# Neighbourhood attention by pairs of heads in row tiles, with a moved first pair and a moved group of channel sums

## The chip, the cores and the metric

The kernel runs on one core of one Trainium2 chip, as a hand-written program for its engines: TensorE (PE, whose weight loads are listed as PEld), VectorE (DVE), ScalarE (ACT), GpSimd (POOL) and SyncE (SP). The metric is the device time of one execution in microseconds; the value shown is the median of several runs.

## The reference, cut to what matters

The whole computation is a hybrid layer (a state-space part and a forgetting attention) on 272 tokens, and then, on 256 tokens, two layers that each hold a convolution module, a neighbourhood attention, a feed-forward part (dense in layer 0, a mixture of eight experts in layer 1) and norms. All is float32. The change touches the two neighbourhood attentions and the channel norm of the convolution that runs between them.

```python
def neighbourhood_attention(q, k, v, rpb):       # 8 heads of 64, a grid of 4 rows of 64 columns
    scale = Dh ** -0.5
    ...
    s = jnp.einsum("bjqhd,bijkhd->bhjqik", q_row, k_band).astype(jnp.float32) * scale
    s = jnp.where(col_mask[:, :, None, :], s + bias.astype(jnp.float32), -jnp.inf)
    w = jax.nn.softmax(s.reshape(B, H, N_CB, Q_CB, kr * BAND_C), axis=-1)
    return jnp.einsum("bhjqik,bijkhd->bjqhd", w, v_band)

def conformer_conv(a, g, w, b, ln_g, ln_b):
    u = a * jax.nn.sigmoid(g)
    y = lax.conv_general_dilated(u, w[:, None, :], ...)   # 31 taps, 512 channels
    y = layer_norm(y + b, ln_g, ln_b)                     # over the 512 channels
    return jax.nn.silu(y)

def hybrid_stack(h):
    for i in range(2):
        proj = h @ w_in[i] + b_in[i]          # a, g, q, k, v of 512 columns each
        conv_out, attn_out = conformer_conv(...), neighbourhood_attention(...)
        mix = jnp.concatenate([conv_out, attn_out], axis=-1) @ w_out[i] + b_out[i]
        h = layer_norm(ALPHA * h + mix, ...)
        ...
```

With 256 tokens in four grid rows every query sees all four rows, so a head's scores for 128 queries are a 128 x 256 tile, to which a table of biases (`tb`, with -1e30 where a column is outside the window) is added.

## The kernel before

Every engine runs its own instruction list in the order in which it is written, and waits on semaphores, which the helper `wait(engine, name, value)` names. `S["x"].on(instruction)` makes an instruction count up semaphore x. There is no scheduler: what stands behind a waiting instruction on an engine waits too. TensorE alone may load weights ahead.

Weights come in chunks of 1 MB through a ring of six places by DMAs that SP issues when TensorE has released a place (`give`, `chunks_used`). Each large product is made of three passes: ACT rounds a chunk to a high part (L1516 and others), DVE makes the rest (L2040), and TensorE multiplies high x high, high x rest, rest x high (`split_product`, listed at L642).

In each of the two layers (`layer(i)` of the three engines) `features` computes the projections of gate, values of the convolution, keys and queries in blocks f of 128 columns: f = 8 to 11 are keys, 12 to 15 queries. ACT's `keys(f)` (L1823, L1827) moves a block out of its bank with its bias. Keys lie in `k2` with two heads per tile of 128 partitions; queries lie in `q2` with one tile per head, of which DVE's `zero_halves` has set the other head's half to zero, so that a score matmul over 128 partitions takes one head. Between blocks 14 and 15 `conv_mean` (L1205) sums the convolution's output over channels; DVE subtracts the mean (L2516) and ACT squares it (L1858).

Then comes the attention, as u = 0 to 15: u // 8 is the half of the queries (128 each), u % 8 the head. For each u:
- TensorE `scores2(u)` (L1217): 128 x 256 scores into one of three banks;
- DVE: scale and add of the bias (L2523), then the negated row maximum (L2527), into one of three places of `sc2`;
- ACT: exponential with the sum over the row (L1863);
- TensorE `turn2(u)` (L1224): two 128 x 128 transposes;
- ACT `copy_t` (L1915): the transposed weights into `p2T`;
- TensorE `weigh2(u)` (listed at L642 with 128x64 outputs): two products with the values.

TensorE's order is a software pipeline: at step u it runs scores2(u), turn2(u - 2), weigh2(u - 3). Into it are put `conv_spread` (L1242, sums of squares over channels, at u = 2), `conv_scale` (L1249, at u = 9), and `turn_a(0)` (L1256, transposes of the first half's output, at u = 15). On DVE the steps that belong to them are an ask for an inverse root to POOL (u == 4), the diagonal tiles (L2535, u == 6), the scaling of the convolution (L2540, u == 10) and `attended(0)`, the division by the row sums (L2509, L2511, u == 11). After the 16 steps come the products with w_out, "the mix", whose first matmul reads the transposed and split first half (`copy_a`, L1870, and `rest_a`, L2547).

The attention of the hybrid layer, earlier in the same kernel, is written in another form, which the diff takes over: `scores(p)` (L940 adds a decay row, L945 the scores) runs two heads as two matmuls over 64 partitions each, on the upper and lower half of the array's rows; DVE does addition, negation and minimum in one `tensor_tensor_reduce` (L2284); `turn_p` (L955) does the transposes of both heads, DVE copies them together (L2294), and `weigh` (L975) follows.

## Time and profile before

| | us |
|---|---|
| median of 3 runs | 2062.36 (2062.07 to 2062.44) |
| the profiled execution | 2061.95 |
| its span | 2060.3 |

| engine | busy us | share of span | instructions |
|---|---|---|---|
| PE | 2035.3 | 99% | 10989 |
| PEld | 1699.0 | 82% | 10989 |
| DVE | 1579.0 | 77% | 1430 |
| ACT | 1269.3 | 62% | 1272 |
| POOL | 163.2 | 8% | 134 |

The granted clock of TensorE is at its full level in all 40 slices of the span. A busy TensorE is not one at its peak, since matmuls overlap and their ends are modelled; what counts is the distance from one start to the next. The chain of waits goes back from the last instruction, at each step to what released it or to the instruction before it on its engine. In a timeline consecutive instructions of a kind are one line with their count.

### The profile page before, as it was taken

The page shows a single profiled execution, that of the slowest core. Times are in us where ns is not written, and L with a number is a line of the kernel's source. Part 1 is how long each engine was busy: PE and PEld are TensorE (multiplying, and loading weights), DVE is VectorE, ACT ScalarE, POOL GpSimd, SP SyncE. Part 2 cuts the span into 40 slices and gives each one's busy share as a digit, 9 for nine tenths or more (in the row PEclk, how much of TensorE's full clock was granted, in tenths as well). Part 3 has the DMA queues.
Part 4 walks back from the last instruction along what each step waited for, and adds up shares of the span by engine and source line. Part 5 has one row for each costly group of instructions (what it writes and reads, how often), then busy time and mean ns, then how long its engine had stood idle before and what let it go on. Part 6 is the DMA issues. An engine that isn't in the chain of part 4 may idle for free.

```text
span 2060.3 us, 29349 instructions
## 1 busy us (share of the span) xinstructions
PE 2035.3 (99%) x10989; PEld 1699.0 (82%) x10989; DVE 1579.0 (77%) x1430; ACT 1269.3 (62%) x1272; POOL 163.2 (8%) x134
## 2 busy tenths in 40 slices
PE   9999999999999999999999999999999999999998
PEld 8977897778889998987778888888888888888876
DVE  7767544687666557679988888888888888888897
ACT  7666433453644334466677777777777777777674
POOL 0031010000214000021400000000000000000100
PEclk9999999999999999999999999999999999999999
DMA  6533594237555555726999999999999999999995
GB/s 254 186 103 105 196 358 169 83 131 261 159 185 202 189 185 187 255 90 228 358 412 383 367 384 370 371 380 368 382 370 381 368 371 380 368 382 370 383 381 211
DMA packets 88065, 580.41 MB, mean 282 GB/s; under 512 B 10144, under 2 KB 13472, under 8 KB 22064
## 3 DMA queue, kind: packets, MB, share of 16 engines
q1 hardware_dynamic: 79472, 548.26, 70.7%
q0 software_dynamic: 7904, 29.95, 4.0%
q8 instruction: 57, 0.93, 0.2%
q10 hardware_dynamic: 608, 1.07, 0.2%
q14 instruction: 24, 0.20, 0.0%
HBM read 559.96 MB, written 15.73 MB: 279 GB/s over the span
## 4 chain that ended last, share of the span: by engine, by line
PE 91%; DVE 4%; DMA 1%; issue 1%; ACT 1%; POOL 0%; DVEq 0%; ACTq 0%; SPq 0%
PE bank L642 84%; PE bank L1414 1%; DMA ring<-in_w_moe 1%; DVE wrest L2634 1%; PE bank L857 1%; PE bank L1217 1%; DVE wrest L2040 0%; DMA cst<-in_consts 0%; PE bank L860 0%; PE bank L1385 0%; PE bank L1031 0%; PE bank L945 0%; PE bank L975 0%; PE bank L1224 0%; ACT ohi L1737 0%
## 5 line engine op out<-in xcount | busy, mean ns | idle before, releaser
L2634 DVE TENSOR_TENSOR wrest<-ring,whi 128x2048 fp32r<-128x2048 f32 x378 | 853.7, 2304 | 77.7 <-ACT whi L1939 77.3
L1939 ACT ACTIVATE whi<-ring 128x2048 fp32r<-128x2048 f32 x374 | 699.2, 1918 | 84.1 <-DMA ring<-in_w_moe 82.0
L642 PE MATMUL bank<-whi,xgT 128*128 128x512 f32 x1008 | 404.7, 402 | 3.0 <-DVE wrest L2634 3.0
L642 PE MATMUL bank<-wrest,xgT 128*128 128x512 f32 x1008 | 396.3, 393 | 0.0
L642 PE MATMUL bank<-whi,xgR 128*128 128x512 f32 x1008 | 393.5, 390 | 0.0
L642 PEld LDWEIGHTS bank<-whi,xgT 128*128 128x128 f32 x1008 | 189.5, 188 | 47.3 <-DVE wrest L2634 7.1
L642 PEld LDWEIGHTS bank<-whi,xgR 128*128 128x128 f32 x1008 | 189.5, 188 | 46.6
L642 PEld LDWEIGHTS bank<-wrest,xgT 128*128 128x128 f32 x1008 | 188.9, 187 | 38.7
L642 PE MATMUL bank<-whi,hidE 128*128 128x512 f32 x504 | 201.8, 400 | 0.8 <-DVE wrest L2634 0.8
L642 PE MATMUL bank<-wrest,hidE 128*128 128x512 f32 x504 | 197.8, 392 | 0.0
L642 PE MATMUL bank<-whi,hidR 128*128 128x512 f32 x504 | 196.8, 390 | 0.0
L642 PE MATMUL bank<-hTh,wrest 128*128 128x256 f32 x608 | 171.4, 282 | 0.0
L1954 ACT ACTIVATE arena<-bank 128x512 f32<-128x512 f32 x63 | 37.6, 597 | 179.1 <-PE bank L642 179.1
L2040 DVE TENSOR_TENSOR wrest<-ring,fhi 128x2048 fp32r<-128x2048 f32 x33 | 76.5, 2317 | 81.8 <-ACT fhi L1516 81.8
L642 PEld LDWEIGHTS bank<-hTh,wrest 128*128 128x128 f32 x608 | 114.6, 188 | 0.0
L642 PEld LDWEIGHTS bank<-whi,hidR 128*128 128x128 f32 x504 | 94.7, 188 | 23.6
L642 PEld LDWEIGHTS bank<-whi,hidE 128*128 128x128 f32 x504 | 94.6, 188 | 22.6 <-DVE wrest L2634 2.3
L1516 ACT ACTIVATE fhi<-ring 128x2048 fp32r<-128x2048 f32 x33 | 63.0, 1913 | 78.0 <-PE bank L642 78.0
L642 PEld LDWEIGHTS bank<-wrest,hidE 128*128 128x128 f32 x504 | 94.4, 187 | 20.1
L2040 DVE TENSOR_TENSOR wrest<-ring,lhi 128x2048 fp32r<-128x2048 f32 x20 | 45.9, 2293 | 71.4 <-ACT lhi L1524 71.4
L642 PE MATMUL bank<-hTh,fhi 128*128 128x256 f32 x352 | 99.4, 282 | 0.0
L642 PE MATMUL bank<-hTr,fhi 128*128 128x256 f32 x352 | 99.0, 281 | 0.0
(483 smaller groups left out, 3688.5 us busy)
## 6 DMA issues: line engine op xcount, KB each, us to landing
ring<-in_w_moe SPq DMA_DIRECT2D x378, 1024.0 KB, 4.9
ring<-in_w_dense SPq DMA_DIRECT2D x135, 1024.0 KB, 4.8
row<-in_rows POOLq DMA_DIRECT2D x17, 512.0 KB, 5.2
xg_rows<-ncR POOLq DMA_DIRECT2D x12, 512.0 KB, 25.2
y_rows<-arena POOLq DMA_DIRECT2D x9, 512.0 KB, 6.2
arena<-xg_rows SPq DMA_DIRECT2D x9, 512.0 KB, 5.4
arena<-arena SPq DMA_DIRECT2D x32, 106.5 KB, 3.8
arena<-in_tbias POOLq DMA_DIRECT2D x2, 1536.0 KB, 8.8
```

Of the source, the lines that this page charges most:

```text
L642: ins = pe.matmul(out_, lhsT, rhs, start=start, stop=stop, **more)
L857: ins = pe.matmul(ps[5][:, r * HD:(r + 1) * HD], dec[:, j, r * P:(r + 1) * P], xdt[:, j, r * HD:(r + 1) * HD], start=True, stop=True, skip ...
L1217: S["s_ps"].on(pe.matmul(score_bank(u), q2[:, hh, j * P:(j + 1) * P], k2[:, hh // 2, :], start=True, stop=True))
L1414: ins = pe.transpose(ps[4][:, b * P:(b + 1) * P], hid[:, b * P:(b + 1) * P], ident)
L1516: S["w_hi"].on(a.activation(hi, ring[:, c % RING, :], ACT.Copy))
L1939: S["w_hi"].on(a.activation(whi[:, n % HI_SLOTS, :], ring[:, c % RING, :], ACT.Copy))
L1954: S["m_sl"].on(a.activation(sle, ps[0][:, :], ACT.Silu))
L2040: S["w_lo"].on(v.tensor_tensor(wrest[:, s, :], ring[:, s, :], hi.bitcast(F32), ALU.subtract))
L2634: S["w_lo"].on(v.tensor_tensor(wrest[:, s, :], ring[:, s, :], whi[:, n % HI_SLOTS, :].bitcast(F32), ALU.subtract))
```

## The change

Four things are changed in both layers. (1) Queries are kept as keys are, two heads per tile, scaled by 1/8 when they are moved out; `zero_halves` is gone, and DVE scales the query bias once. Scores, transposes and weighings go by pairs p = 0 to 7: two score matmuls over 64 partitions in row tiles, four transposes into one bank, one copy of 128 x 512, four products. (2) On DVE one `tensor_tensor_reduce` takes the place of two operations, into four places; the copies of pairs 0, 1, 3, 6, 7 are DVE's, those of 2, 4, 5 ACT's. (3) The scores of pair 0 stand between the query blocks 14 and 15, behind `conv_mean`; on ACT `keys(15)` is moved behind the first two exponentials. (4) `conv_spread` is moved from before the first transposes to behind the weighing of pair 0; the steps of the norm on DVE move to u = 6, 8, 11 and `attended(0)` to u = 13.

```diff
@@ -59,6 +59,7 @@
 START_FILL = 12
+DVE_COPIES, ACT_COPIES = (0, 1, 3, 6, 7), (2, 4, 5)
 AHEAD = 4
@@ -245,8 +246,8 @@
         cc, rdiag = at(9792, 4, SEQ), at(24064, 2, P)
-        k2, q2, v2 = at(10816, 4, SEQ), at(11840, N_HEADS, SEQ), at(26624, 2, 512)
-        sc2, p2T, o2 = at(13888, 3, SEQ), at(14656, 2, SEQ), at(15168, 2, 512)
+        k2, q2, v2 = at(10816, 4, SEQ), at(11840, 4, SEQ), at(26624, 2, 512)
+        sc2, p2T, o2 = at(12864, 4, SEQ), at(13888, 2, 512), at(15168, 2, 512)
         tb = at(16384, N_HEADS, 6 * GRID_W)
@@ -394,6 +395,12 @@
             return 5 * (q + 1)
+
+        def copied(i, p):
+
+            for name, copies, first in (("pt_done", DVE_COPIES, meta_count(3)), ("t_done", ACT_COPIES, 0)):
+                if p in copies:
+                    return name, first + len(copies) * i + copies.index(p) + 1
@@ -1205,33 +1212,44 @@
-                features(14, 16, conv_mean)
-                wait(pe, "p_act", 12 * i + 11)
-
-
-                def scores2(u):
-                    j, hh = divmod(u, N_HEADS)
-                    if u == 2:
+                def scores2(p):
+                    if p == 1:
                         wait(pe, "cn_done", 3 * i + 1)
-                    wait(pe, "s_in", 16 * i + max(u - 2, 0))
-                    S["s_ps"].on(pe.matmul(score_bank(u), q2[:, hh, j * P:(j + 1) * P], k2[:, hh // 2, :],
-                                           start=True, stop=True))
-
-                def turn2(u):
-                    wait(pe, "s_exp", 16 * i + u + 1)
-                    wait(pe, "t_done", 16 * i + max(u - 1, 0))
-                    for b in range(2):
-                        ins = pe.transpose(ps[2 + u % 2][:, b * P:(b + 1) * P], sc2[:, u % 3, b * P:(b + 1) * P],
-                                           ident)
+                    wait(pe, "s_in", 16 * i + max(2 * p - 1, 0))
+                    for u in (2 * p, 2 * p + 1):
+                        j, hh = divmod(u, N_HEADS)
+                        r = slice(HD * (u % 2), HD * (u % 2) + HD)
+                        S["s_ps"].on(pe.matmul(score_bank(u), q2[r, hh // 2, j * P:(j + 1) * P], k2[r, hh // 2, :],
+                                               start=True, stop=True))
+
+                def conv_mean_and_scores():
+                    conv_mean()
+                    wait(pe, "p_act", 12 * i + 10)
+                    scores2(0)
+
+                features(14, 16, conv_mean_and_scores)
+
+
+                def turn2(p):
+                    wait(pe, "s_exp", 16 * i + 2 * p + 2)
+                    if p >= 2:
+                        wait(pe, *copied(i, p - 2))
+                    for u in (2 * p, 2 * p + 1):
+                        for b in range(2):
+                            x = 2 * (u % 2) + b
+                            ins = pe.transpose(ps[2 + p % 2][:, x * P:(x + 1) * P], sc2[:, u % 4, b * P:(b + 1) * P],
+                                               ident)
                     S["t_ps"].on(ins)
...
-                def weigh2(u):
-                    j, hh = divmod(u, N_HEADS)
-                    c = slice(hh * HD, (hh + 1) * HD)
-                    wait(pe, "t_done", 16 * i + u + 1)
-                    for b in range(2):
-                        ins = mm(ps[4 + j][:, c], p2T[:, u % 2, b * P:(b + 1) * P], v2[:, b, c],
-                                 start=b == 0, stop=b == 1, skip_group_check=True)
+                def weigh2(p):
+                    wait(pe, *copied(i, p))
+                    for u in (2 * p, 2 * p + 1):
+                        j, hh = divmod(u, N_HEADS)
+                        c = slice(hh * HD, (hh + 1) * HD)
+                        for b in range(2):
+                            x = 2 * (u % 2) + b
+                            ins = mm(ps[4 + j][:, c], p2T[:, p % 2, x * P:(x + 1) * P], v2[:, b, c],
+                                     start=b == 0, stop=b == 1, skip_group_check=True)
                     S["a_ps"].on(ins)
@@ -1256,23 +1274,24 @@
-                for u in range(19):
-                    if u == 3:
-                        wait(pe, "p_act", 12 * (i + 1))
-                    if u < 16:
-                        scores2(u)
-                    if u == 2:
-                        conv_spread()
-                    if u == 9:
+                for p in range(1, 10):
+                    if p in (2, 3):
+                        wait(pe, "p_act", 12 * i + 9 + p)
+                    if p < 8:
+                        scores2(p)
+                    if p == 5:
                         conv_scale()
-                    if u == 15:
+                    if p == 8:
                         wait(pe, "cn_done", 3 * (i + 1))
                         turn_a(0, 7)
-                    if 2 <= u <= 17:
-                        turn2(u - 2)
-                    if u >= 3:
-                        weigh2(u - 3)
-                wait(pe, "t_done", 16 * (i + 1))
+                    if p <= 8:
+                        turn2(p - 1)
+                    if p >= 2:
+                        weigh2(p - 2)
+                    if p == 2:
+                        conv_spread()
+                wait(pe, *copied(i, 6))
+                wait(pe, *copied(i, 7))
                 wait(pe, "s_in", 16 * (i + 1))
@@ -1822,10 +1841,8 @@
                     else:
-                        for e in range(2):
-                            r = slice(e * HD, (e + 1) * HD)
-                            ins = a.activation(q2[r, 2 * (f - 12) + e, :], ps[f % 4][r, 0:SEQ], ACT.Identity,
-                                               bias=bias[r])
+                        ins = a.activation(q2[:, f - 12, :], ps[f % 4][:, 0:SEQ], ACT.Identity, bias=bias,
+                                           scale=HD ** -0.5)
                     S["p_act"].on(ins)
@@ -1856,14 +1873,15 @@
                 S["cq_done"].on(a.activation(csq[:, :, :], cc[:, :, :], ACT.Square))
-                keys(15)
                 for u in range(16):
+                    if u == 2:
+                        keys(15)
                     j, hh = divmod(u, N_HEADS)
                     wait(a, "s_in", 16 * i + u + 1)
-                    S["s_exp"].on(a.activation(sc2[:, u % 3, :], sc2[:, u % 3, :], ACT.Exp,
+                    S["s_exp"].on(a.activation(sc2[:, u % 4, :], sc2[:, u % 4, :], ACT.Exp, scale=-1.0,
                                                bias=nmax[:, u % 4:u % 4 + 1], accum_out=rsum[:, j, hh:hh + 1]))
-                    if u:
-                        copy_t(i, u - 1)
+                    if u % 2 == 0 and u // 2 - 1 in ACT_COPIES:
+                        copy_t(i, u // 2 - 1)
@@ -1879,7 +1897,6 @@
                 copy_a(0, 7)
-                copy_t(i, 15)
                 wait(a, "cn_done", 3 * (i + 1))
@@ -1909,10 +1926,10 @@
-            def copy_t(i, u):
-                wait(a, "t_ps", 16 * i + u + 1)
-                wait(a, "a_ps", 16 * i + max(u - 1, 0))
-                S["t_done"].on(a.activation(p2T[:, u % 2, :], ps[2 + u % 2][:, 0:SEQ], ACT.Copy))
+            def copy_t(i, p):
+                wait(a, "t_ps", 8 * i + p + 1)
+                wait(a, "a_ps", 8 * i + max(p - 1, 0))
+                S["t_done"].on(a.activation(p2T[:, p % 2, :], ps[2 + p % 2][:, :], ACT.Copy))
@@ -2204,12 +2221,6 @@
                 S["t_lo"].on(v.tensor_tensor(yTr[:, t, :], yT[:, t, :], yTh[:, t, :].bitcast(F32), ALU.subtract))
-
-            def zero_halves(q):
-
-                pairs = q[:, :, :].rearrange("p (f e) n -> p f e n", e=2)
-                v.memset(pairs[HD:P, :, 0, :], 0.0)
-                fin(v.memset(pairs[0:HD, :, 1, :], 0.0))
@@ -2476,7 +2487,8 @@
                 rest_proj(i, 4)
-                zero_halves(q2)
+                q_bias = vec[:, v0 + VL_BK + 4:v0 + VL_BK + 8]
+                v.tensor_scalar(q_bias, q_bias, HD ** -0.5, None, ALU.mult)
                 rest_proj(i, 5)
@@ -2507,7 +2519,7 @@
                     fin(v.reciprocal(rinv[:, j, 0:8], rsum[:, j, 0:8]))
-                    wait(v, "a_ps", 16 * i + 8 * (j + 1))
+                    wait(v, "a_ps", 8 * i + 4 * (j + 1))
                     S["a_ready"].on(v.tensor_tensor(o2[:, j, :].rearrange(c3, r=8), ps[4 + j][:, :].rearrange(c3, r=8),
@@ -2516,31 +2528,37 @@
                 v.wait_ge(tb_in, 16 * (i + 1))
+                def copy_t(p):
+                    wait(v, "t_ps", 8 * i + p + 1)
+                    wait(v, "a_ps", 8 * i + max(p - 1, 0))
+                    S["pt_done"].on(v.tensor_copy(p2T[:, p % 2, :], ps[2 + p % 2][:, :]))
+
                 for u in range(16):
...
                     wait(v, "s_ps", 16 * i + u + 1)
-                    wait(v, "t_ps", 16 * i + max(u - 2, 0))
-                    fin(v.scalar_tensor_tensor(sc2[:, u % 3, :], score_bank(u), HD ** -0.5,
-                                               tb[:, hh, (2 - 2 * j) * GRID_W:(6 - 2 * j) * GRID_W],
-                                               ALU.mult, ALU.add))
+                    wait(v, "t_ps", 8 * i + max(u // 2 - 1, 0))
                     wait(v, "s_exp", 16 * i + max(u - 3, 0))
-                    S["s_in"].on(v.tensor_reduce(nmax[:, u % 4:u % 4 + 1], sc2[:, u % 3, :], AX.X, ALU.max,
-                                                 negate=True))
-                    if u == 4:
+                    S["s_in"].on(v.tensor_tensor_reduce(sc2[:, u % 4, :], score_bank(u),
+                                                        tb[:, hh, (2 - 2 * j) * GRID_W:(6 - 2 * j) * GRID_W], -1.0, 3e38,
+                                                        ALU.add, ALU.min, nmax[:, u % 4:u % 4 + 1]))
+                    if u % 2 and u // 2 - 1 in DVE_COPIES:
+                        copy_t(u // 2 - 1)
+                    if u == 6:
                         wait(v, "cv_ps", 3 * i + 2)
                         asked = ask_inv_sqrt(rs[:, 6:8], ps[7][:, 0:2], 1.0 / CONV_CH, LN_EPS)
-                    if u == 6:
+                    if u == 8:
                         wait(v, "pow_done", asked)
...
                         S["cn_done"].on(ins)
-                    if u == 10:
+                    if u == 11:
                         wait(v, "cv_ps", 3 * i + 3)
...
                                                          ALU.mult))
-                    if u == 11:
+                    if u == 13:
                         attended(0)
+                copy_t(7)
                 def rest_a(j, bank):
```

## Rows read from the trace of the kernel before

**Rows 1.** The page, part 4: the chain that ended last, by engine.
```profile
PE 91%; DVE 4%; DMA 1%; issue 1%; ACT 1%; POOL 0%; DVEq 0%; ACTq 0%; SPq 0%
```

**Rows 2.** Chain of waits about layer 0's attention: start us, length us, what.
```profile
482.16 59.35 PE bank L642 x576
...
543.24 2.85 PE bank L642 x24
...
547.39 1.68 PE bank L1242 x16
...
554.62 0.39 PE bank L642 x4
555.02 0.49 PE bank L1217 x2
555.50 0.22 PE bank L1224 x2
...
556.60 0.43 PE bank L1249 x2
...
571.34 16.65 PE bank L642 x72
```

**Rows 3.** The same chain in layer 1.
```profile
877.41 2.85 PE bank L642 x24
...
905.50 16.65 PE bank L642 x72
```

**Rows 4.** Timeline, layer 0: start us, length, engine, line, operation [idle before <-releaser].
```profile
544.67 1.06 ACT L1858 ACTIVATE arena<-arena 128x1024 f32<-128x1024 f32 x1 [2.17 <-DVE arena L2516]
...
547.10 1.28 ACT L1863 ACT_TABLE_LOAD   x1
...
562.62 0.51 ACT L1863 ACTIVATE arena<-arena,nmax 128x256 f32<-128x256 f32 x1 [0.75 <-DVE nmax L2527]
...
563.27 0.44 PE L1224 MATMUL bank<-cst,arena 128*128 128x128 f32 x2 [0.21 <-ACT arena L1863]
...
567.88 0.47 PE L642 MATMUL bank<-aside,catH 128*128 128x512 f32 x1
```

**Rows 5.** Groups by form, 538 to 572 us: busy us, mean ns | idle before, releaser.
```profile
L2523 DVE SCALAR_TENSOR_TENSOR arena<-bank,arena 128x256 f32<-128x256 f32 x16 | 6.7, 421 | 5.1 <-PE bank L1217 5.0
...
L2527 DVE TENSOR_REDUCE nmax<-arena 128x1 f32<-128x256 f32 x16 | 6.7, 420 | 0.6
...
L1827 ACT ACTIVATE arena<-bank,vec 64x256 f32<-64x256 f32 x4 | 1.9, 470 | 0.8 <-PE bank L642 0.8
```

**Rows 6.** Timeline of the first block's attention, which is by pairs in row tiles.
```profile
399.26 0.73 PE L945 MATMUL bank<-arena 64*128 64x272 f32 x4
399.93 0.66 PE L955 MATMUL bank<-cst,arena 128*128 128x128 f32 x4
400.02 0.44 DVE L2284 CUSTOM_DVE_ANT_0 arena<-bank,causal 128x272 f32<-128x272 f32 x1 [0.70 <-PE bank L945]
...
400.42 1.00 PE L975 MATMUL bank<-arena 128*128 128x64 f32 x8
400.51 0.52 ACT L1720 ACTIVATE arena<-arena,nmax 128x272 f32<-128x272 f32 x1 [1.68 <-DVE nmax L2284]
...
400.75 0.69 DVE L2294 COPY arena<-bank 128x512 f32<-128x512 f32 x1
...
401.03 0.51 ACT L1720 ACTIVATE arena<-arena,nmax 128x272 f32<-128x272 f32 x1
...
401.23 0.50 PE L940 MATMUL bank<-ncR,picked 128*128 128x272 f32 x2
```

**Rows 7.** By line: its durations, min/median/max ns.
```profile
L945 PE MATMUL bank<-arena x64: 282/388/493, 373.6 to 413.2; 64*128 64x144 f32 x32, 64*128 64x272 f32 x32
...
L1710 ACT ACTIVATE yaTh<-bank x4: 576/577/582, 396.2 to 426.5; 128x512 fp32r<-128x512 f32 x4
...
L2569 DVE TENSOR_TENSOR arena<-arena,bank x8: 686/688/690, 579.8 to 926.6; 128x512 f32<-128x512 f32 x8
```

## Prediction

> **What bounds the kernel now.** I read the page's chain first: 91% of it is TensorE [rows 1], so an edit counts only as far as it shortens TensorE's own sequence or a gap in it. Next the chain of waits around the place that changes. Before it, TensorE runs one unbroken stretch of 59.35 us [rows 2], so ACT or DVE work that is saved there (the two memsets of zero_halves, the halved `keys` activations of queries) buys nothing: it lies beside that stretch. From 543.24 the last query block takes 2.85 us, and from 546.09 to 567.88, when the first matmul of the mix starts [rows 2, 4], comes the neighbourhood attention: 21.79 us. In layer 1 the distance from the last query block (877.41) to the long mix stretch (905.50) is 28.09 us; in layer 0 it is 571.34 - 543.24 = 28.10 [rows 2, 3]. So one calculation does for both layers.
>
> Inside, a head costs TensorE 0.49 (score) + 0.22 (two transposes) + 0.39 (weighing) = 1.10 us [rows 2]. Sixteen heads are 17.60; the sums of squares take 1.68, conv_scale 0.43 [rows 2] and turn_a four transposes, 0.44: together 20.15. The remaining 1.64 us are gaps, late in the stage, where DVE's two operations per head and its conv work make it late: 5.0 us of DVE's idle time wait for scores [rows 5], and an exponential starts after 0.75 us of ACT idling, with the transposes behind it 0.65 later [rows 4].
>
> **The change, part by part.** The best witness for the new form is the first block's attention, which already runs by pairs in row tiles, with the same one-pass DVE operation.
>
> Scores. Two K=64 matmuls of four instructions at 272 columns take 399.93 - 399.26 = 0.67 from first start to the transposes [rows 6]; with 256 columns an estimate of 0.64. That is more than half of two full-array scores (0.98, [rows 2]), so the tiles overlap only in part. Bounds: 0.49 (full overlap) and 0.98 (none).
> Transposes. Four take 400.42 - 399.93 = 0.49, weighing a pair 401.23 - 400.42 = 0.81 [rows 6], against 0.44 and 0.78 for two heads now: grouping is slightly dearer here. A pair costs 0.64 + 0.49 + 0.81 = 1.94 against 2.20; eight pairs 15.52 against 17.60, so 2.08 us of TensorE work go per layer. The other 2.55 us stay.
>
> The Trainium skill, TensorEngine Tiling (Array Packing), Key Properties, speaks against the change: "Changing tiling mode (not just tile) drains the TensorE". I make it the slower rival below. The page TensorE: Matmul & The Clock Gate, Part 3, says that row tiles start a few ns apart; by that a pair's scores would cost about half of the serial price. The row's 0.67 does not show this, and as the next lines show ACT's round trip would then set the pace, so the sum would move by some tenths only.
>
> DVE. Before, 0.42 + 0.42 per head [rows 5]; after, one pass: from the first to the copy behind the second 400.75 - 400.02 = 0.73 for two [rows 6], 0.36 each. DVE takes on five pair copies of 0.69 [rows 6] per layer. Its sum falls by 16 x 0.48 - 3.5 = 4.2 us, and it drops out as the late engine. ACT loses sixteen copies and gains three of 0.58 [rows 7]. q_bias adds one four-column DVE operation in the covered stretch: nothing. The asks for the inverse root, and with them POOL's power and residual, move two heads later; their reader on DVE first runs at 579.8 [rows 7], some 12 us after the stage: nothing. No DMA is moved, and the SP queue follows TensorE's releases.
>
> The new waits. transposes(p) now wait for both exponentials of pair p. From the start of a pair's scores: 0.73 to DVE (0.76 at 272 columns), 0.46 to ACT (0.49), 0.50 to the second exponential (0.52) [rows 6], 0.65 to the transposes [rows 4]: 2.34. TensorE comes there by itself after 1.94 + 0.64 = 2.58: no gap. When ACT has a copy between the two exponentials (pairs 3, 5, 6 see this), another 0.50 (its length is 0.58): 2.84, so a gap of 0.26; for pair 5 conv_scale's 0.43 fills it. What is queued behind the waiting transposes is the weighing of the pair before, which was ready.
>
> The start. Moving the first scores costs TensorE nothing extra, and DVE can take them after the centring, about 544.66, while the last query block runs. ACT has the square until 545.73 and then the table load of 1.28 [rows 4]: exponentials at 547.04 and 547.55, so the first transposes can start at 548.20. TensorE is there at 547.37: gap 0.83. Before, conv_spread stood there and filled this; now it stands behind weigh(0). Then `keys(15)` (0.47 at half width [rows 5], 0.4 to the next start) is queued between exponentials 1 and 2, so exponentials 2 and 3 start at 548.56 and 549.06, transposes(1) at 549.71 at the earliest, TensorE is there at 549.33: 0.38.
>
> The schedule of layer 0 that follows (start times of scores, transposes, weighing of the pair before; S0 at 543.24, query block until 546.73):
>
> | | scores | transposes | weighing | then |
> |---|---|---|---|---|
> | p=1 | 546.73 | 548.20 (gap 0.83) | | |
> | p=2 | 548.69 | 549.71 (0.38) | 550.20 | spread to 552.69 |
> | p=3 | 552.69 | 553.33 | 553.82 | |
> | p=4 | 554.63 | 555.53 (0.26) | 556.02 | |
> | p=5 | 556.83 | 557.90, after conv_scale | 558.39 | |
> | p=6 | 559.20 | 559.84 | 560.33 | |
> | p=7 | 561.14 | 562.04 (0.26) | 562.53 | |
> | p=8 | | 563.78, after turn_a | 564.27 | |
> | p=9 | | | 565.27 (0.19) | mix at 566.08 |
>
> The last gap: the copy of pair 7 starts between 0.49 and 0.82 after its transposes [rows 6] (I take 0.75) and runs 0.69 plus 0.05. The split of the first half of the heads (`rest_a`), which the mix needs first, is on DVE right behind this copy and ends before 566.08; ACT's SiLU chain starts 1.4 us ahead of the mix where it was 0.5 ahead. So TensorE is late next, and the shift of 567.88 - 566.08 = 1.80 us is kept. Gaps are 1.92 against 1.64: of the 2.08 saved, 0.28 are given back. Behind the stage the chain is 16.65 us of unbroken matmuls in both layers [rows 2, 3] and what loads weights is released by TensorE, so everything shifts by 1.80 x 2 = 3.6 us.
>
> The profiled execution took 2061.95 (span 2060.3), the median of the runs is 2062.36, 0.4 above; the saving is the same for both. I take it from the median: 2062.36 - 3.6 = 2058.8.
>
> **The rivals.**
> Fewer gaps. If the round trip to ACT is shorter than read, or the last matmuls hide the starts, the gaps go: per layer at most 1.80 + 1.92 = 3.72, in all 7.4, 2054.9. For it: ACT and DVE both have less to do. Against: the table load and the exponentials cannot start earlier than the square, so 0.8 of it is firm. A likely size is half, 2057.0.
> No gain. If row tiles don't overlap, scores cost 0.98 a pair instead of 0.64: 8 x 0.34 = 2.7 a layer, reduced by the gaps of 0.26, 0.26 and part of the others, which then are hidden: about +2.1, more than the 1.80. With 0.86 in the middle it is unchanged: 2062.3. Against: the 0.67 of the first block. The same end is reached if the change doesn't do what it says, that is, if ACT and DVE wait for each other over the copies, 0.25 us more in seven of eight pairs.
> Slower by draining. Scores of a pair switch from 128 to 64 rows and back: 16 switches a layer, 32 in all. A matmul of this kind lasts up to 0.493 [rows 7] while its share of the pair is 0.17 to 0.23, so a full drain costs an estimated 0.26: 8.3 us against 3.6 saved, 2067.1. It decides from 3.6/32 = 0.11 us per switch. Against: going back to full width shows only 0.49 against 0.44 for four transposes, 0.05, already in the sum. Entering from a weighing is not shown before, since a full-array matmul stands between; this keeps the rival alive.
>
> **How the numbers follow.** Forecast as summed, 2057.6 to 2060.5: 0.63. Fewer gaps, 2054.9 to 2057.6: 0.17. No gain, 2060.5 to 2062.9: 0.14. Slower by draining or something like it: 0.06. This kernel's measurement tells about 0.2% from no change, 4.1 us, so the bound for faster is 2058.2, inside my forecast's own range: of its 0.63 about 0.21 lies below. Faster 0.21 + 0.17 = 0.38; same 0.42 + 0.14 = 0.56, slower 0.06. The range reaches to the bounds of the gaps and to most of the no-gain case: 2056.0 to 2061.4.
>
> **What would show it.** In the profile after: the row-tiled score group with 0.64 us between the first score of a pair and its transposes, and no tail; the one-pass DVE group near 0.42 mean; a gap of 0.8 us in front of the first transposes, named for the exponential, and 0.4 before the second; the mix 22.8 us behind the start of scores(0), in both layers; no growth of waits behind it. Wrong would be the forecast if the transposes of most pairs, not only those with an ACT copy in between, wait for exponentials, if the first matmul of a weighing or of a score takes a quarter us more than its neighbours, or if the mix then waits for DVE.

## The result, and the profile after

The changed kernel takes 2073.52 us (median of 20 runs, 2063.64 to 2082.73) against 2062.21 for the kernel before (20 runs on the same chip, 2061.58 to 2062.81): a ratio of 1.0054, 95% interval 1.0041 to 1.0068. It is slower, by 11.3 us in the medians, where 2058.8 was forecast and 2061.4 was the upper end. The profiled execution took 2074.01, its span is 2072.3.

The spread of its own runs is a hint: 19.1 us, where the kernel before has 1.2. Each run also lists the mean granted TensorE clock of its span. Three runs at 2063.6 to 2063.9 have 0.996, five at 2067.7 to 2068.9 have 0.994, five at 2072.5 to 2075.0 have 0.991 or 0.992, one each at 2077.8 and 2079.8 have 0.989 and 0.987, and five at 2082.0 to 2082.7 have 0.986. Time and clock lie on one line.

So the first view is the page of the kernel after, part 2, the row of the granted clock in 40 slices (a digit is tenths of the full clock; 9 is 90% or more). Before, it was 9 in all of them.

```profile
PEclk9999999999999999989999999999999999999999
```

The eighteenth slice, 881 to 932 us, has an 8; it holds layer 1's attention. The page's chain, which answers to [rows 1], has the same 91% for TensorE and says nothing of it:

```profile
PE 91%; DVE 4%; ACT 2%; DMA 1%; issue 1%; POOL 0%; DVEq 0%; SPq 0%; ACTq 0%
```
The next view is the table of stretches, here of the kernel after (stretch, length; busy us of PE, PEld, DVE, ACT and POOL, each with its count of records, of which some can be missing; granted clock, share of DMA, GB/s).

```profile
541.00:552.00 11.00, 10.31 (x76) 8.38 (x74) 6.92 (x16) 7.10 (x17) 0.00 (x0) 1.00 0.26 95
552.00:554.00 2.00, 2.00 (x18) 1.59 (x17) 0.00 (x0) 0.00 (x0) 0.00 (x0) 0.95 0.84 279
554.00:564.00 10.00, 9.92 (x43) 7.84 (x41) 6.97 (x17) 3.64 (x12) 9.18 (x5) 0.50 0.10 43
564.00:566.00 2.00, 2.00 (x17) 1.60 (x17) 0.95 (x4) 0.98 (x4) 1.75 (x1) 0.99 0.00 0
...
892.00:912.00 20.00, 20.00 (x87) 16.64 (x86) 7.54 (x26) 8.39 (x25) 10.85 (x5) 0.50 0.02 7
```

The same stretches of the kernel before:

```profile
554.00:564.00 10.00, 9.57 (x66) 7.98 (x66) 8.68 (x22) 6.74 (x25) 9.15 (x4) 1.00 0.05 20
...
892.00:912.00 20.00, 19.47 (x113) 16.05 (x112) 13.46 (x23) 15.14 (x33) 5.36 (x3) 1.00 0.00 1
```

The granted clock, 1.00 or 0.50 behind the five busy times, is what the forecast left out. In the attention of both layers TensorE is granted half of its clock, 1.2 GHz for 2.4: in this execution for 10.24 us in layer 0 and 20.48 us in layer 1, by the trace's record of the clock. And PE's busy time does not show it: 9.92 of 10 us, more than before. Only the counts do, 43 matmul records in 10 us for 66. From the scores of the first pair to the first matmul of the mix layer 0 takes 571.63 - 543.75 = 27.88 us, and layer 1 32.31, where 22.84 was forecast.

What it does to a pair is seen in the chain of waits of the kernel after in layer 1 (start us, length us, what): scores, transposes and weighing of one pair take 1.16, 1.04 and 1.60.

```profile
893.57 1.16 PE bank L1222 x4
894.72 1.04 PE bank L1240 x4
895.77 1.60 PE bank L649 x8
```

TensorE's timeline of the kernel after in layer 0 shows how far the forecast's schedule came true (start us, length, ... [idle before <-releaser]; L1222 are the row-tiled scores, L1240 the transposes, L1260 the sums of squares):

```profile
543.75 0.70 PE L1222 MATMUL bank<-arena 64*128 64x256 f32 x4
...
547.43 0.70 PE L1222 MATMUL bank<-arena 64*128 64x256 f32 x4
548.77 0.66 PE L1240 MATMUL bank<-cst,arena 128*128 128x128 f32 x4 [0.64 <-ACT arena L1881]
...
551.45 1.90 PE L1260 MATMUL bank<-cst,arena 128*128 128x1 f32 x16
553.27 0.77 PE L1222 MATMUL bank<-arena 64*128 64x256 f32 x4
553.97 1.11 PE L1240 MATMUL bank<-cst,arena 128*128 128x128 f32 x4
...
571.63 0.48 PE L649 MATMUL bank<-aside,catH 128*128 128x512 f32 x1
```

Counted from the scores of pair 0, the third pair's transposes start at 10.22 us, forecast 10.09; from there the transposes last 1.11 for 0.66. By the trace's record the clock fell at 553.78, and in layer 1 at 891.70, shortly after the sums of squares. TensorE had then run for 5 us without a gap of more than 0.1 us. DVE and ACT did what was planned. The groups by form in 543 to 572 us, which answer to [rows 5] (busy us, mean ns | idle before, releaser), in the kernel after:

```profile
L2541 DVE CUSTOM_DVE_ANT_0 arena<-bank,arena 128x256 f32<-128x256 f32 x16 | 6.3, 419 | 9.3 <-PE bank L1222 9.3
...
L2534 DVE COPY arena<-bank 128x512 f32<-128x512 f32 x5 | 3.4, 689 | 1.6 <-PE bank L1240 1.6
```

DVE has one pass of 419 ns per head where it had two of 421 and 420, and waits 9.3 us for scores where it waited 5.0: TensorE is the late engine, as forecast. The clock has only a part in that: in the kernel with wide sums below, at full clock, DVE waits 7.6.

### The profile page after: what moved, and what is told of

Same layout as the page of the kernel before. It is cut to its first block, busy times and chain, and to the rows that moved or that the text cites. A ratio compares the mean times of both kernels' runs of the same rounds, so it can differ in the third digit from the quotient of the medians.

```text
span 2072.3 us, 29262 instructions
## 1 busy us (share of the span) xinstructions
PE 2046.9 (99%) x10989; PEld 1704.6 (82%) x10989; DVE 1571.2 (76%) x1438; ACT 1257.6 (61%) x1238; POOL 159.4 (8%) x134
## 4 chain that ended last, share of the span: by engine, by line
PE 91%; DVE 4%; ACT 2%; DMA 1%; issue 1%; POOL 0%; DVEq 0%; SPq 0%; ACTq 0%
PE bank L649 83%; DMA ring<-in_w_moe 1%; PE bank L1433 1%; DVE wrest L2652 1%; PE bank L864 1%; DVE wrest L2057 1%; PE bank L1240 0%; PE bank L752 0%; PE bank L1222 0%; PE bank L867 0%; PE bank L1404 0%; PE bank L1038 0%; PE bank L952 0%; PE bank L982 0%; ACT arena L1881 0%
```

## The experiments

The theory after this look: the change lowers what the array does in the attention, and the granted clock falls for it. It has two parts: matmuls with one moving column are moved between pairs that are thin already (theory A in the expectations), and scores use half of the array's rows (theory B). The rivals: the new gaps ahead of the first transposes let it fall (theory C); or the order alone costs the time, without the clock. Each kernel was timed in five rounds beside the kernel before.

**The sums of squares back in front of the first transposes.**

```diff
                     if p < 8:
                         scores2(p)
+                    if p == 1:
+                        conv_spread()
...
-                    if p == 2:
-                        conv_spread()
```

> The changed kernel with one move undone: conv_spread stands again before the first transposes (behind scores(1)), the rest is as changed. The changed kernel's profile shows TensorE at 1.2 GHz for 10.24 us in layer 0's attention and for 20.48 us in layer 1's; over its 20 runs the time and the mean granted clock move together (2063.6 at 0.996, 2082.7 at 0.986), and the line through them reaches the clock of the kernel before (0.9986) at about 2059. Theory A (the one-column sums, moved into a stretch that is thin anyway, let the clock fall): here the full clock holds in both attentions, mean clock 0.998 to 0.999, time 2057 to 2060, little spread. Theory B (row-tiled scores use half of the array, and that lets it fall): the clock falls as before, 2064 to 2083. Theory C (the gap of 0.6 and 0.3 us in front of the first two groups of transposes lets it fall): the sums fill the gap, so as with A.

Median 2064.6, ratio 1.002 (0.9991 to 1.0049). The 12 runs fall apart: five at 2057.3 to 2057.9 with clock 0.999, three at 2064.2 to 2065.0 (0.995), one at 2072.1, three at 2080.4 to 2084.4 (0.984 to 0.986). The profiled one fell for 30.72 us in layer 0 and not at all in layer 1; its stretches:

```profile
554.00:564.00 10.00, 9.91 (x41) 7.31 (x40) 5.43 (x12) 2.67 (x8) 7.71 (x4) 0.50 0.30 105
...
898.00:908.00 10.00, 9.93 (x76) 7.75 (x74) 6.67 (x24) 6.71 (x23) 8.09 (x4) 1.00 0.30 107
```

Same code in both layers: 41 records in one, 76 in the other. None of the three expectations came: the clock neither held in all runs (A and C) nor fell in all (B). So the place of the sums shifts how often the clock falls, but it can fall without it. It falls without gaps as well: in this profile TensorE has none of more than 0.1 us in either attention. In the five runs in which it doesn't fall, this kernel is 4.6 us faster than before, which speaks against the rival of the order alone.

**Scores over all 128 rows.** The pairs, the order and the count of instructions are kept; each score matmul now contracts over the channels of both heads, so it computes the sum of the two heads' scores instead of each head's own.

```diff
-q2[r, hh // 2, j * P:(j + 1) * P], k2[r, hh // 2, :]
+q2[:, hh // 2, j * P:(j + 1) * P], k2[:, hh // 2, :]
```

> The changed kernel with full-array scores in the same order and number: each score matmul contracts over all 128 partitions of its tile, so it adds the scores of both heads of a pair (this part of the computation is changed; its time is that of scores without row tiles). A pair's scores cost 0.98 us where they cost 0.66. Theory B (row tiles): the full clock holds, time 2061 to 2065. Theory A (the place of the one-column sums) and theory C (the gap): the clock falls in both attentions, mean clock 0.986 to 0.996, time 2066 to 2087, as widely spread as the changed kernel.

2061.82 (11 runs, 2059.48 to 2065.16), ratio 0.9997 (0.9989 to 1.0006), clock 0.997 to 0.999. Its profile has one stretch of 3.41 us at half clock, in layer 1. Its scores, by TensorE's timeline, take 0.91 from start to start:

```profile
554.98 1.08 PE L1222 MATMUL bank<-arena 128*128 128x256 f32 x4
555.89 0.60 PE L1240 MATMUL bank<-cst,arena 128*128 128x128 f32 x4
```

That is 0.28 more per pair than row tiles (0.63), and still the whole kernel is 11.7 us faster than the changed one. With full rows the clock hardly falls, and in this profile it comes back sooner. That is theory B's expectation; A's and C's did not come.

**The kernel before, with the sums late.** Single heads over 128 rows, no row tiles; only conv_spread is moved.

```diff
-                    if u == 2:
-                        conv_spread()
...
                     if u >= 3:
                         weigh2(u - 3)
+                    if u == 3:
+                        conv_spread()
```

> The kernel before with one part of the change alone: conv_spread moved from before the first transposes to behind the first weighing. Scores stay full-array and by single heads. Moving it opens a gap of about 1.7 us in front of the first transposes (they waited until 549.05, TensorE is there at 547.39), of which later waits give some back. Theory A: the clock falls in at least some of the runs, time 2066 to 2085. Theory B: the clock holds, 2063 to 2066, the gap alone. Theory C: falls, as with A, perhaps more, since the gap is longer than in the changed kernel.

2071.68 (5 runs, 2069.87 to 2074.59), ratio 1.0045 (1.0032 to 1.0058), clock 0.995 to 0.997. Its profile has 3.41 us twice in layer 0 and 6.83 us in layer 1 at half clock. So moving the sums is enough to lose clock, without a single row tile. The first kernel lost it with row tiles and the sums at their old place: neither half of the change is the only cause. Not all of the 9.5 us is clock: in layer 0 of this profile TensorE also waits 0.98 us ahead of conv_scale and 0.72 ahead of the next transposes, for reasons that the kernel with a wait, below, shows.

**Wide sums.** The changed kernel, its order untouched; the sums of squares are taken against 128 columns of ones instead of one, so 16 matmuls move 128 columns where they moved one.

```diff
-ps[7][:, j:j + 1], csq[:, f, j * P:(j + 1) * P], ones[:, 0:1]
+ps[7][:, j * P:(j + 1) * P], csq[:, f, j * P:(j + 1) * P], ones
-ps[7][:, 0:2], 1.0 / CONV_CH, LN_EPS
+ps[7][:, 0:2 * P:P], 1.0 / CONV_CH, LN_EPS
```

> The changed kernel with one size changed: the sums of squares multiply by 128 columns of ones instead of one, in the same place, with the same 16 weight loads, which set their pace at 0.11 us each, so the stretch stays 1.7 to 1.8 us long. The result is the same in each column. Theory A in its narrow form (the one-column matmuls leave the array idle though TensorE is busy): the clock holds, 2057 to 2060. Theories B and C: the clock falls as in the changed kernel, 2064 to 2083.

2059.25 (11 runs, 2058.56 to 2060.14), ratio 0.9986 (0.9977 to 0.9995), clock 0.998 or 0.999 in all 11, no stretch at half clock in its profile but the last 6 us of the span. Every kernel here has that one, of 4 to 7 us, the kernel before too; the slices of the page are too long to show it. The sums take 1.93 instead of 1.82 and the kernel is 14.3 us faster for it. This is the clock theory's cleanest witness: the order and the number of instructions are untouched, and the sums themselves became longer. The stretch that was at half clock, in this kernel:

```profile
554.00:564.00 10.00, 9.86 (x77) 7.78 (x74) 6.90 (x28) 6.37 (x20) 8.89 (x5) 1.00 0.12 52
```

PE is busy 9.86 of 10 us here and 9.92 there; 77 records and 43. The expectation of theory A came; B and C had expected a fall.

**Both: sums first and wide.** The edits of the first and the fourth kernel together.

> The changed kernel with two edits: conv_spread back in front of the first transposes, as in e1_spread_first, and its matmuls with 128 columns of ones, as in e4_wide_spread. Without a fall of the clock e1 took 2057.3 to 2057.9, and with wide sums in the late place the clock held in all 11 runs of e4 (2058.6 to 2060.1). Theory D (no single edit lets the clock fall; it falls when a stretch of the attention has too few streamed columns in sum, and the one-column sums are its largest hole): the clock holds in all runs, 2057 to 2058.5, faster than both kernels. Rival (the place decides: where the sums stand between full-array matmuls and thin pairs the fall comes with some phase anyway): a part of the runs at 2064 or more, as in e1.

2057.92 (11 runs, 2056.96 to 2058.32), ratio 0.9977 (0.9968 to 0.9986), clock 0.998 or 0.999 in all. As expected, the clock held in all runs. This is the fastest of the study, below both kernels by more than the measurement's uncertainty. Its chain in layer 0:

```profile
547.31 0.63 PE bank L1222 x4
547.94 1.98 PE bank L1260 x16
549.92 0.44 PE bank L1240 x4
```

The sums fill the gap ahead of the first transposes, which is what the kernel before did with them. The first kernel's five undisturbed runs, 2057.3 to 2057.9, agree with it.

**Half the rows alone.** The kernel before, single heads in its own order, each score over its head's own 64 partitions.

```diff
-q2[:, hh, j * P:(j + 1) * P], k2[:, hh // 2, :]
+q2[HD * (u % 2):HD * (u % 2) + HD, hh, j * P:(j + 1) * P],
+k2[HD * (u % 2):HD * (u % 2) + HD, hh // 2, :]
```

> The kernel before with one part of the change alone: each score matmul takes only the 64 partitions of its own head (the other half, zeros, is left out), still by single heads, so no two run beside each other. Everything else, the place of the sums too, is as before. Price without the clock: each of 16 scores a layer goes into and out of row tiling; from e4's profile a weighing followed by row-tiled scores takes 0.93 where the schedule had 0.81, so about 0.12 to 0.2 us a head, partly hidden: 2064 to 2068. Theory B (row tiles alone let the clock fall): 2070 or more with a clock below 0.996 in most runs. Theory D: the sums here stand in the same place as before, next to full blocks, so few or no falls; clock 0.997 to 0.999.

2102.12 (5 runs, 2101.22 to 2103.78), ratio 1.0192 (1.0179 to 1.0205), clock 0.979 or 0.980: the worst. It is at half clock for 40.96 us in each layer, from the first heads on (550.20 in layer 0), though the sums are at their old place. Theory B had expected a fall, but not its size; theory D, stated with the kernel before this one, that there would be few or none. Chain of layer 0 (L1217 the score, L1224 the transposes, L642 the weighing of one head), and then the stretch in which the clock falls and a later one:

```profile
552.22 1.15 PE bank L1217 x2
553.37 0.62 PE bank L1224 x2
553.99 0.75 PE bank L642 x4
```
```profile
544.00:554.00 10.00, 9.98 (x60) 7.85 (x59) 4.87 (x11) 6.14 (x14) 0.00 (x0) 0.81 0.13 29
...
564.00:574.00 10.00, 10.00 (x33) 7.00 (x31) 4.80 (x10) 3.56 (x12) 1.55 (x1) 0.50 0.00 0
```

A head costs 2.52 us for 1.10 before. PE is busy 9.98 of 10.00 us in the stretch in which the clock falls, and 10.00 of 10.00 later. The edit does two things that no run here takes apart: it halves the rows in use, and it makes the array switch between row tiles and full rows at every head. Nor is it row tiles as such: the first block's attention, by pairs in row tiles in every kernel of this document [rows 6], has the full clock in all profiles (396 to 413 us, PE busy 16.84 of 17 us in the kernel before).

**Gaps filled.** The changed kernel with matmuls of 256 columns that nobody reads: two ahead of the first transposes, one ahead of the second.

```diff
+                    if p == 1:
+                        for _ in range(2):
+                            pe.matmul(ps[7][:, 0:SEQ], ident, cst[:, 0:SEQ], ...)
+                    if p == 2:
+                        pe.matmul(ps[7][:, 0:SEQ], ident, cst[:, 0:SEQ], ...)
                     if p <= 8:
                         turn2(p - 1)
```

> The changed kernel with matmuls that nobody reads put into its two gaps: two of 256 columns (0.43 us each) before the first transposes, one before the second, the one-column sums in their late place as changed. Theory C (the gaps let the clock fall): it holds, 2059 to 2060. Theory D: the fall begins about 553.9, over 3 us after the gaps have ended, with the sums in between; it still comes in most runs, perhaps later or shorter, 2063 to 2083.

2070.64 (9 runs, 2064.27 to 2073.84), ratio 1.0039 (1.0027 to 1.0051), clock 0.991 to 0.996. The gaps are gone, the fall is not: in its profile layer 0 kept the clock, layer 1 did not.

```profile
554.00:564.00 10.00, 9.87 (x77) 8.04 (x77) 7.26 (x28) 6.72 (x22) 9.25 (x5) 1.00 0.11 47
...
888.00:898.00 10.00, 9.93 (x46) 7.78 (x44) 6.70 (x14) 4.17 (x14) 9.83 (x5) 0.54 0.03 11
```

So the gaps are not needed for a fall, as the first kernel has shown too. Whether they have a small part is open: the median is 2.9 us lower, inside the spread of both, and none of 9 runs is above 2073.9, where 7 of the changed kernel's 20 are at 2077 or more.

**A wait put in on purpose.** The kernel with wide sums, with DVE's two scalings of the identity (`rdiag`) two heads later.

```diff
-                    if u == 8:
+                    if u == 10:
                         wait(v, "pow_done", asked)
```

The profile of the kernel after had shown a second oddity, in its timeline of DVE and POOL: two operations that had taken 0.47 together took 3.44 in layer 0, and the first of them alone 2.44.

```profile
558.22 3.44 DVE L2552 TENSOR_SCALAR arena<-cst,rs 128x128 f32<-128x128 f32 x2
558.23 2.34 POOL L554 TENSOR_TENSOR arena<-arena,row 128x1024 f32<-128x1024 f32 x1
```

Before, the two ran beside another POOL operation, one with one input, and took 0.47 together:

```profile
552.89 2.79 POOL L545 TENSOR_SCALAR arena<-h 128x1024 f32<-128x1024 f32 x1
...
554.14 0.47 DVE L2535 TENSOR_SCALAR arena<-cst,rs 128x128 f32<-128x128 f32 x2
```

> The kernel of e4_wide_spread with the diagonal tiles of the norm (two DVE operations of 0.28 us) moved from u == 8 to u == 10. In three profiles (changed kernel, e1_spread_first, e3_before_late) the first of the two took 2.4 us in layer 0, each time when POOL's two-input addition had started within 0.02 us of it; beside POOL's one-input scaling it took 0.28. At u == 10 it should start at about 559, inside POOL's addition (558.5 to 560.9). Theory L (DVE waits for the end of POOL's two-input operation): the first takes 1.5 to 2.4 us in layer 0, conv_scale and what stands behind it on TensorE wait, and the time rises by 1.5 to 4 us over e4's 2059.3. Rival (the 2.4 us belong to the low TensorE clock, at which all three were): 0.28 us each, the time rises by less than 1.5 us, from the later place alone.

2082.25 (4 runs, 2080.82 to 2083.3), ratio 1.0093 (1.0079 to 1.0108), clock 0.989 to 0.991: 23.0 us over the kernel with wide sums, where at most 4 were expected. The timeline shows DVE held by POOL, and that this begins at full clock:

```profile
557.66 2.34 POOL L554 TENSOR_TENSOR arena<-arena,row 128x1024 f32<-128x1024 f32 x1
...
558.09 3.00 DVE L2552 TENSOR_SCALAR arena<-cst,rs 128x128 f32<-128x128 f32 x2
...
561.14 1.22 PE L1267 MATMUL bank<-arena,cst 128*128 128x256 f32 x2 [3.43 <-DVE arena L2552]
```

The first scaling ends at 560.08, just after POOL's addition at 560.00. When the clock falls, at 559.37, it has lasted 1.28 us already, where it takes 0.28 elsewhere. So the long scalings were no effect of the slow clock. But the price is far above the wait itself: conv_scale waits 3.43 us for DVE, and the clock is at half for 20.48 us in each layer, wide sums or not. It falls 1.66 us after TensorE has stopped (1.64 in layer 1), with the rest of the gap still to come. So waiting in the attention is a second way to lose the clock, but how long a gap it takes is not shown: the next kernel has one of 1.66 us, at another place, and keeps its clock. Gaps of 0.6 us, as the change makes them, are not shown to be one.

**The kernel before, sums late and wide.** The third kernel with the fourth one's edit.

> The kernel before, single heads, with the sums of squares behind the first weighing as in e3, but each summed against 128 columns of ones. Clock theory (the thin one-column matmuls moved behind the first heads' work let TensorE's granted clock fall, row tiles or not): with wide sums no piece at half clock, 9.3 us less than e3 in its runs' middle only as far as the clock goes: what is left over the kernel before is the gap ahead of the first transposes, about 1.0 us a layer less the 1.7 us that the sums filled there, so 2063 to 2065.5. Rival (the place of the sums is not what counts, the idle gap before the first transposes is): the clock still falls for 3.4 to 7 us in a layer, 2068 to 2074.

2065.66 (11 runs, 2064.64 to 2066.62), ratio 1.0017 (1.0008 to 1.0026), clock 0.998 or 0.999 in all. The stretch of 552 to 566 us with one-column sums, the third kernel:

```profile
552.00:566.00 14.00, 12.29 (x68) 10.32 (x68) 9.47 (x18) 6.17 (x21) 10.95 (x5) 0.81 0.20 73
```

and with wide ones, this kernel:

```profile
552.00:566.00 14.00, 13.57 (x97) 11.67 (x95) 10.88 (x28) 8.67 (x29) 10.95 (x5) 1.00 0.18 71
```

Both have the same gap of 1.66 us ahead of the first transposes. So this gap does not lose the clock, and width alone gives it back. The 3.5 us that stay over the kernel before (the expectation ended at 2065.5) are about this gap, twice 1.66, which the sums filled before.

**The kernel before, sums wide at their own place.**

> The kernel before with nothing changed but the sums of squares against 128 columns of ones instead of one, at their own place. Clock theory: the kernel before has lost no clock, so width gains nothing: 2061.5 to 2063, within 0.1% of before; the sums take 1.85 us instead of 1.68 and part of the 0.2 lies ahead of exponentials that come late anyway. Rival (wide sums help by something else, such as ones' columns loaded or a faster reader): 1 us or more below before, as between e1's and g1's runs.

2062.11 (11 runs, 2061.75 to 2063.09), ratio 1.0 (0.9991 to 1.0009). Where no clock is lost, width gains nothing, so the fourth and fifth kernels' gain is not some other merit of wide sums.

The medians together, in us, with what the clock did by the mean clock of each run:

| | sums thin, first | thin, late | wide, late | wide, first |
|---|---|---|---|---|
| single heads, 128 rows | 2062.2, no fall | 2071.7, falls | 2065.7, no fall | 2062.1, no fall |
| pairs, row tiles | 2064.6, falls in 7 of 12 runs | 2073.5, falls in all 20 | 2059.2, no fall | 2057.9, no fall |

## Why the prediction was wrong

The step that failed stands in no term of the sum: every duration in it was read at the full clock, and it was taken without a word that the new order would be granted the same. The runs showed half of the clock instead: in the profiled one for 10.24 and 20.48 us in the two attentions, and in all 20 a mean clock below that of the kernel before. None of the three rivals is about the clock, so the range could not hold what came. Rows of before could have raised the question (the attention's matmuls are short, and the change halves the rows of some and puts 16 one-column matmuls between them), but no row of before shows a fall there, so they could not have given its price. The witness for the new form, the first block's row-tiled pairs, even ran at the full clock.

Point by point, with the kernel with wide sums as the witness at full clock. Its timeline in layer 0:

```profile
542.17 1.89 PE L1212 MATMUL bank<-arena,cst 128*128 128x256 f32 x8
...
543.99 0.70 PE L1222 MATMUL bank<-arena 64*128 64x256 f32 x4
...
549.01 0.66 PE L1240 MATMUL bank<-cst,arena 128*128 128x128 f32 x4 [0.65 <-ACT arena L1881]
...
553.62 0.70 PE L1222 MATMUL bank<-arena 64*128 64x256 f32 x4
554.25 0.66 PE L1240 MATMUL bank<-cst,arena 128*128 128x128 f32 x4
554.75 1.00 PE L649 MATMUL bank<-arena 128*128 128x64 f32 x8
555.68 0.70 PE L1222 MATMUL bank<-arena 64*128 64x256 f32 x4
...
563.74 1.00 PE L649 MATMUL bank<-arena 128*128 128x64 f32 x8
564.58 0.61 PE L1274 MATMUL bank<-cst,arena 128*128 128x128 f32 x4
...
567.32 0.48 PE L649 MATMUL bank<-aside,catH 128*128 128x512 f32 x1
```

- **Scores of a pair**: 554.25 - 553.62 = 0.63, forecast 0.64. Transposes 0.50, forecast 0.49. Right.
- **Weighing**: 555.68 - 554.75 = 0.93, forecast 0.81. In front of turn_a's full-array transposes the same weighing takes 564.58 - 563.74 = 0.84. So entering row tiles from a weighing costs 0.09 us, in this layer four times; the draining rival was real and a third of its 0.26, below the 0.11 from which it would have decided.
- **The first gap**: first transposes 5.02 after scores 0, forecast 4.96. The chain square, table load, exponential was right.
- **Other terms**: the gaps, counted as the forecast does, are 0.72, 0.13, 0.14, 0.14 and 0.18, in all 1.31 us a layer, forecast 1.92. Against that the prediction took some lengths from the chain of waits as if they were distances between starts. The timeline of the kernel before has 545.93 - 542.89 = 3.04 for the last query block, where the chain has 2.85, and 549.05 - 547.23 = 1.82 for the sums, where it has 1.68.
- **The whole attention**: 567.32 - 543.99 = 23.33, forecast 22.84. The prediction's 24.64 for the kernel before, from 543.24 to 567.88, mixes a start in the chain with one in the timeline. In the timeline alone, counted from `conv_mean`, which is the same in both kernels, it is 567.88 - 541.35 = 26.53 before and 567.32 - 542.17 = 25.15 here. So 1.38 us a layer are saved of the forecast's 1.80: twice 1.38 is 2.8, and 2062.2 - 2.8 = 2059.4; measured 2059.25. This is near the forecast's 2058.8, in part by luck, since costs that were too small and gaps that were too large nearly cancel.

The start in the timeline of the kernel before:

```profile
541.35 1.89 PE L1205 MATMUL bank<-arena,cst 128*128 128x256 f32 x8
```

- **ACT, DVE, the queues**: nothing became late by itself, as forecast. But moving the asks two heads later was costed at nothing with the cover of DVE's late reader; the operation that mattered was `rdiag`, which then met POOL's two-input addition in layer 0. At half clock this hid behind TensorE, but for 0.80 us in which the weight load of conv_scale waited.
- **The clock**: nearly the whole difference, 14.3 of the 14.7 us between 2073.52 and the forecast. At half clock a pair costs 1.16 + 1.04 + 1.60 = 3.80 for 2.06. The runs of the kernel after lie on a line from 2063.75 at a clock of 0.996 to 2082.3 at 0.986, that is 1.86 us for 0.001; carried on to the 0.998 to 0.999 of the kernel before, this is 2060.0 to 2058.2, where the forecast stood. That number is worked out, not measured: none of the 20 runs kept the clock.

The Trainium skill, TensorE: Matmul & The Clock Gate, Part 4: PE-mode transpose, says that transposes don't count as busy for the clock gate as matmuls do. No run here tells a transpose from a matmul in this. The same page of the Trainium skill, Part 1, HAM oscillation, tells of clock lost in idle gaps. In the kernel with the wait a fall does come with a gap of 3.43 us, though 1.66 us after its start; the kernel of half rows does not fit, since it fell with PE busy 9.98 of 10.00 us.

What stays open: what exactly the chip counts. The runs show that columns moved, a long wait, and either the rows in use or the switching between row tiles and full rows all matter, not by which measure. In the profiles falls with row tiles last longer (10.24 to 40.96 us, against 3.41 to 6.83 with 128 rows). Why equal code falls in one layer and one run and not in the next (the first kernel) is open too.

## What to carry to other kernels

When matmuls are split into row tiles or one-column matmuls are moved between small ones, read the granted clock of that stretch, in several runs, and not PE's busy share, which stays at 99%: the clock lost for 10.24 us in layer 0 cost 4.6 us (27.88 for 23.33), more than the 1.4 us a layer that the change saves. If a clock is lost that way, give the thin matmuls more columns, since 128 columns cost hardly more than one (1.93 us for 1.82), and put them where TensorE would idle. Mind what a small delay on another engine does to TensorE there: one of 3.4 us a layer cost 23 us in all. Time such a change by a dozen runs: groups some us apart with different clocks are its mark.

## What the runs showed of the hardware

- The granted clock can fall to 1.2 GHz while TensorE is busy without a break, and stay there: with single heads on 64 rows it falls in a stretch with PE busy 9.98 of 10.00 us, and stays for 40.96 us in each layer, at a cost of 39.9 us.
- One-column matmuls take nearly the time of 128-column ones, 1.82 and 1.93 us for 16 of them; between small matmuls they differ in the clock that follows (below full in all 20 runs, full in all 11).
- A DVE operation with one input of 128x128 takes 0.28 us, and 2.44 in the kernel after, where it starts 0.01 us before POOL's two-input TENSOR_TENSOR. Started 0.09 us before such an addition it took its 0.28 (layer 1 of the kernel with full rows). Beside POOL's one-input TENSOR_SCALAR two of them took 0.47 together, 1.25 us after that had begun; one that started 0.03 us after its beginning took 1.08, in the kernel after and in the one with the wait. The Trainium skill, SBUF — State Buffer, "SBUF: two separate sides", calls the shared port pair an exclusive lock that goes to whichever starts first, while the other blocks entirely. The trace agrees for the two-input addition (in the kernel with the wait it ends at 560.00 and DVE's operation at 560.08, and only the 0.01 us of the kernel after goes against the order of starts), and for the one-input operation only in part, since by that rule the lock would have held those 0.47 as well.
- Four fp32 score matmuls in row tiles take 0.63 us against 0.91 on all rows: 0.28 us are saved of the 0.46 that full overlap in pairs would save. Entering row tiles from a full-array weighing costs 0.09 us.
